# One transformer layer on one core: three groups of blocks, each group's mixer woven into the expert gathers of the group before, and gathered tiles of 4 picks by 32 tokens

## The chip, the cores and the metric

The kernel runs on one core of a Trainium2 chip. The metric is the device time of one execution in microseconds; lower is better. The engines are named as the profile names them: PE is the matrix engine TensorE (PEld its weight loads), DVE is VectorE, ACT is ScalarE, POOL is GpSimd, SP is the engine that issues plain DMAs.

## What is computed

1024 tokens of width 1024, float32. The first half of the layer is the mixer, the second half a retrieval of single-neuron experts (PEER).

```python
mod = silu(c) @ w_ada + b_ada                        # 6 rows of 1024
h = rmsnorm(x, g1) * (1 + scale1) + shift1
qa, ka, va, qb, kb, vb, ga, gb = split(h @ w_in)
y_sb = stick_breaking_attention(qa, ka, va)          # 8 heads, strictly causal: block b reads blocks 0..b
y_sw = sliding_window_sink_attention(qb, kb, vb)     # each chunk of 64 reads itself and the one before
merged = sigmoid(ga) * (y_sb @ sb_proj) + sigmoid(gb) * (y_sw @ sw_proj)
x = x + gate1 * (merged @ w_out)
h2 = rmsnorm(x, g2) * (1 + scale2) + shift2
q = h2 @ w_q                                         # 8 heads x 2 halves of 128
s = q . sub_keys ; top 16 of 128 in each half; top 16 of the 256 sums -> 16 expert numbers, softmax gates
out_t = sum over 8 heads x 16 picks of gate * gelu(h2_t . U[e]) * V[e]     # U, V: 16384 x 1024
x = x + gate2 * out ; final rmsnorm
```

U and V lie side by side in memory (`uv`), so one pick of one token is one row of 8 KB. 1024 tokens x 128 picks x 8 KB are 1074 MB.

## The kernel before

The work stands in stages, one after the other, each for all 8 blocks of 128 tokens: modulation and first norm; stick-breaking attention, a loop over 4 pairs of heads (lines 340 to 510); sliding-window attention (lines 530 to 700); gates, branch projections and merging (to line 773); output projection, residual, second norm and the store of the residual x1 (to line 871); then the experts.

In the stick-breaking loop a chunk is one block of keys against up to 512 later tokens. TensorE makes scores (L462, L466), VectorE splits them into a positive part and a magnitude (L401, L407), ScalarE takes exp and ln (L367, L369), VectorE adds (L418) and keeps a running sum (L429, L432), TensorE adds suffix sums in PSUM (L490, L495), ScalarE takes exp (L377), and TensorE multiplies by the values (L474). Six banks and `AHEAD = 4` keep several chunks under way.

The experts' stage is a loop over the 8 heads. In one turn 128 gathers are made, one for each block b and pick k: POOL's indirect DMA (L950) brings, for the 128 tokens of block b, each token's own row of 8 KB into one of `RING = 8` buffers, a token to a partition. VectorE multiplies the U half by h2 and sums (L1187, `dot`), ScalarE takes the gelu (L1055) and makes a 128x128 diagonal matrix of gate times gelu (L1044, L1060), TensorE multiplies that diagonal with the V half, 1024 columns, and adds up in PSUM (L994):

```python
pe.wait_ge(diag_done, LED + t * PICKS + n + 1)
for i in range(2):
    m = pe.matmul(pb[:, 4 + 2 * (b % 2) + i, :], dg[:, n % 4, :],
                  ring[:, n % RING, D + i * HALF:D + (i + 1) * HALF], start=(k == 0), stop=(k == TOPK - 1))
m.then_inc(ring_free, 1)
```

`ring_free` lets POOL issue the gather that is 8 further on. After 16 picks VectorE adds the block's sum to `acc` (L1176). Between the gathers of head t stand, by a list of fixed places, the keys of head t+1: 32 query matmuls (L966), scores (L975), the top 16 of 128 for 8 blocks and 2 halves (L1097 to L1105, five instructions each), the 256 sums and their top 16, and the decoding of the expert numbers. Head 0's keys stand ahead of the loop (L1007 to L1171). At the end a short stage adds x1 and makes the last norm (L1273, L1284).

Every engine runs its instructions in the order written and waits on semaphores; most stages are hardware loops.

## Time and profile before

| | |
|---|---|
| median of 2 runs | 4077.22 us (4073.49 to 4080.95) |
| span of the profiled execution, first to last instruction | 4068.1 us |
| ahead of the first gather's product | 1347.7 us |
| 1024 gathers and their sums | 2680 us |
| behind them | 40 us |
| busy share of the span | PE 83%, DVE 54%, ACT 27%, POOL 30% |

The profiled execution's span is 9.1 us under the median of the runs; what lies around the span (launch and end) is in the runs' time alone. The first 1347.7 us move few bytes and are TensorE's; the rest moves 1074 MB and keeps the DMA engines full. A busy share over the whole span mixes the two.

### The profile page before, as it was taken

The page shows a single profiled execution, that of the slowest core. Times are in us where ns is not written, and L with a number is a line of the kernel's source. Part 1 is how long each engine was busy: PE and PEld are TensorE (multiplying, and loading weights), DVE is VectorE, ACT ScalarE, POOL GpSimd, SP SyncE. Part 2 cuts the span into 40 slices and gives each one's busy share as a digit, 9 for nine tenths or more (in the row PEclk, how much of TensorE's full clock was granted, in tenths as well). Part 3 has the DMA queues.
Part 4 walks back from the last instruction along what each step waited for, and adds up shares of the span by engine and source line. Part 5 has one row for each costly group of instructions (what it writes and reads, how often), then busy time and mean ns, then how long its engine had stood idle before and what let it go on. Part 6 is the DMA issues. An engine that isn't in the chain of part 4 may idle for free. (4 is left out here: it accounts for less than half of the span.)

```text
span 4068.1 us, 34945 instructions
## 1 busy us (share of the span) xinstructions
PE 3381.3 (83%) x8576; PEld 1494.4 (37%) x8576; DVE 2195.0 (54%) x4545; ACT 1102.9 (27%) x3167; POOL 1206.8 (30%) x1050
## 2 busy tenths in 40 slices
PE   8999999799994777788697788778779778877775
PEld 3444445544442333333242333333324233332321
DVE  2233442310135677478558657747856865765555
ACT  1233330200011223333332332333333232332322
POOL 0000001200001344344344434434435443443442
PEclk9999998999997899998999999999999899999998
DMA  7100000110011799999999999999999999999997
GB/s 312 60 16 0 15 11 0 73 47 31 17 71 77 293 393 408 388 412 392 411 379 400 421 390 399 411 386 409 399 407 396 395 422 384 388 414 414 421 421 323
DMA packets 160296, 1159.90 MB, mean 285 GB/s; under 512 B 17985, under 2 KB 19025, under 8 KB 24689
## 3 DMA queue, kind: packets, MB, share of 16 engines
q0 software_dynamic: 147696, 1074.80, 64.7%
q1 hardware_dynamic: 12418, 83.40, 5.3%
q14 instruction: 156, 1.28, 0.1%
q8 instruction: 26, 0.43, 0.0%
HBM read 1149.74 MB, written 8.39 MB: 285 GB/s over the span
## 5 line engine op out<-in xcount | busy, mean ns | idle before, releaser
L994 PE MATMUL pb<-arena,dg 128*128 128x512 f32 x4096 | 1982.7, 627 | 578.3 <-ACT dg L1060 573.7
L1187 DVE CUSTOM_DVE_ANT_0 arena<-arena 128x1024 f32<-128x1024 f32 x1024 | 1239.4, 1222 | 792.4 <-DMA arena<-in_uv,idx_cur 757.7
L950 POOL DMA_INDIRECT arena<-in_uv,idx_cur x1024 | 1154.4, 1127 | 1609.4 <-PE pb L994 1406.0
L994 PEld LDWEIGHTS pb<-arena,dg 128*128 128x128 f32 x4096 | 785.4, 199 | 1722.0 <-issue 882.3
L1055 ACT ACTIVATE gl<-dots 128x2 f32<-128x2 f32 x512 | 104.0, 203 | 1630.0 <-DVE dots L1187 1624.6
L1060 ACT ACTIVATE dg<-idg,gl 128x128 f32<-128x128 f32 x1024 | 361.7, 395 | 136.3 <-PE pb L994 81.0
L1044 ACT ACTIVATE idg<-ident,gate_cur 128x128 f32<-128x128 f32 x1024 | 346.7, 387 | 0.2
L966 PE MATMUL pb<-arena 128*128 128x512 f32 x448 | 234.4, 605 | 6.0 <-DMA sks<-in_sk 6.0
L741 PE MATMUL pb<-arena 128*128 128x512 f32 x512 | 223.9, 599 | 7.3 <-DMA arena<-in_w_mg 7.3
L770 DVE TENSOR_TENSOR arena<-arena,pb 128x512 f32<-128x512 f32 x32 | 22.0, 687 | 320.4 <-PE pb L748 320.4
L548 POOL MEMSET arena<- 128x512 f32 x1 | 0.5, 524 | 596.8 <-POOLq L345 596.8
L941 POOL MEMSET arena<- 128x8192 f32 x1 | 6.9, 6924 | 477.1 <-POOLq L793 477.1
L741 PEld LDWEIGHTS pb<-arena 128*128 128x128 f32 x512 | 98.4, 192 | 131.1 <-issue 131.1
L966 PEld LDWEIGHTS pb<-arena 128*128 128x128 f32 x448 | 87.1, 195 | 116.1 <-issue 116.1
L446 PE MATMUL pb<-arena 128*128 128x512 f32 x256 | 112.6, 601 | 1.6 <-ACTq L93 1.6
L821 PE MATMUL pb<-arena 128*128 128x512 f32 x256 | 111.1, 593 | 2.6 <-PEq L722 2.6
L748 PE MATMUL pb<-arena 128*128 128x512 f32 x256 | 111.2, 592 | 0.0
L391 DVE COPY arena<-pb 128x512 f32<-128x512 f32 x8 | 5.5, 691 | 194.2 <-PE pb L455 194.2
L286 PE MATMUL pb<-arena 128*128 128x512 f32 x192 | 90.8, 629 | 12.5 <-DMA arena<-in_w_ada 12.5
L401 DVE TENSOR_SCALAR arena<-pb 128x512 f32<-128x512 f32 (+2 forms) x96 | 53.5, 557 | 83.2 <-PE pb L466 48.7
L1176 DVE TENSOR_TENSOR arena<-arena,pb 128x1024 f32<-128x1024 f32 x64 | 77.9, 1217 | 28.2 <-PE pb L994 28.1
L377 ACT ACTIVATE arena<-pb 128x512 f32<-128x512 f32 (+2 forms) x96 | 47.1, 490 | 168.8 <-PE pb L495 135.5
(166 smaller groups left out, 2473.4 us busy)
## 6 DMA issues: line engine op xcount, KB each, us to landing
arena<-in_w_ada SPq DMA_DIRECT2D x12, 2048.0 KB, 12.3
arena<-in_uv,idx_cur POOLq DMA_INDIRECT x1024
arena<-in_w_mg SPq DMA_DIRECT2D x8, 1536.0 KB, 6.3
arena<-in_w_q SPq DMA_DIRECT2D x8, 1024.0 KB
arena<-in_w_sb SPq DMA_DIRECT2D x4, 1536.0 KB, 6.2
arena<-in_x SPq DMA_DIRECT2D x1, 4096.0 KB, 24.4
arena<-in_w_out SPq DMA_DIRECT2D x1, 4096.0 KB, 19.6
arena<-in_x SPq DMA_DIRECT2D x8, 512.0 KB, 7.1
```

The source lines that it names most:

```text
L286: pe.matmul(pb[:, j % 4, :], cb[:, k, :], w[:, k, :], start=(k == 0), stop=False)
L446: m = pe.matmul(pb[:, i, :], wsb[:, i // 2, k, :], hT[:, k, (i % 2) * HALF:(i % 2 + 1) * HALF], start=(k == 0), stop=(k == KT - 1))
L741: m = pe.matmul(pb[:, q, :], wmg[:, u, (q // 2) * KT + k, :], hT[:, k, (q % 2) * HALF:(q % 2 + 1) * HALF], start=(k == 0), stop=(k == KT - 1))
L748: m = pe.matmul(pb[:, 4 + q, :], wmg[:, u, 16 + (q // 2) * 4 + k, :], y[:, k, (q % 2) * HALF:(q % 2 + 1) * HALF], start=(k == 0), stop=(k ...
L821: m = pe.matmul(pb[:, 2 * (b % 2) + i, :], mergedT[:, k, b * P:(b + 1) * P], wout[:, k, i * HALF:(i + 1) * HALF], start=(k == 0), stop=(k ...
L950: pool.indirect_dma_start(ring[:, n % RING, :], None, uv, bass.IndirectOffsetOnAxis(ap=idx_cur[:, n:n + 1], axis=0)).then_inc(gathered[n % ...
L966: m = pe.matmul(pb[:, half, :], wq[:, p, k, :], h2T[:, k, half * HALF:(half + 1) * HALF], start=(k == 0), stop=(k == KT - 1))
L994: m = pe.matmul(pb[:, 4 + 2 * (b % 2) + i, :], dg[:, n % 4, :], ring[:, n % RING, D + i * HALF:D + (i + 1) * HALF], start=(k == 0), stop=( ...
L1044: act.activation(idg[:, n % 4, :], ident[:], ACT.Copy, scale=gate_cur[:, n:n + 1]).then_inc(idg_done, 1)
L1055: act.activation(gl[:, 0:2], dots[:, n % RING:n % RING + 2], ACT.Gelu).then_inc(gelu_done, 1)
L1060: act.activation(dg[:, m % 4, :], idg[:, m % 4, :], ACT.Copy, scale=gl[:, m - n:m - n + 1]).then_inc(diag_done, 1)
L1187: dve.tensor_tensor_reduce(u, h2[:, b, :], u, 1.0, 0.0, ALU.mult, ALU.add, dots[:, n % RING:n % RING + 1]).then_inc(dots_done, 1)
```

## The change

The 8 blocks are split in three groups of 2, 3 and 3 blocks (`GROUPS`). The mixer, the keys and the norm of a group are made for that group alone (256 or 384 tokens wide). Group 0's mixer runs ahead; group 1's is woven into the gathers of group 0's experts, group 2's into the gathers of group 1's; group 2's gathers have nothing beside them but their own top-16 work. The keys and values of the stick-breaking heads of earlier groups go to memory and are read back (`k_dram`, `v_dram`), as do x1, h2 and the modulation rows.

The weaving is written out: nothing is a hardware loop any more. The engines' programs are generated by Python generators that yield at the same points on every engine. A slot is half a quad, that is 2 gathered tiles; `slots_at` deals the 144 pieces of group 1's mixer over 108 slots and the 168 pieces of group 2's over 172 slots, in proportion to the costs in `plan`, and leaves the last `LEAD = 20` slots of each group free. In the plan's proportions group 1's mixer has 3.2 slots for the norm, 37.4 for the stick-breaking heads (40 chunks), 13.8 for the window, 21.3 for the merge, 11.9 for the output and 20.6 for the queries; group 2's has 4.3, 74.7 (64 chunks), 18.9, 29.4, 16.3 and 28.3.

The weights are read in 66 parts of 512 KB (128x1024) for each group, so three times in all, plus 48 parts of `w_ada` once. Ahead of the gathers 14 parts fit in the ring's buffers (`EARLY`), later 4 (`LATE`).

A gathered tile now holds 4 picks of 32 tokens. Its sum needs a 128x32 matrix in place of the 128x128 diagonal, and 4 matmuls of 256 columns, each into another 32 of PSUM's 128 partitions, so into another group of 32 columns of TensorE's array. VectorE's product needs the 32 tokens' h2 four times over (`h2r`, by 16 DMAs a block, `copies`). The tokens' expert numbers and gates must be spread over partitions (`shf`, 16 small copies on ScalarE for each 2 heads) and the 128x32 masks are made 32 at a time on VectorE (`gm`). The ring has 10 buffers.

Two places show the weaving. On PE, in the stick-breaking part of group 1's mixer, names: `wts` the 128x32 weights of a tile, `negones`, `tri` the suffix sums, `zone` the mixer's scratch. Before, in the gathers of a turn's start:

```order
L966 MATMUL pb<-arena 128x512
L992 REGISTER_ALU
L994 MATMUL pb<-arena,dg 128x512 x2
L966 MATMUL pb<-arena 128x512
L992 REGISTER_ALU
L994 MATMUL pb<-arena,dg 128x512 x2
```

Now, one quad (two slots) there:

```order
L841 MATMUL pb<-ring,wts 32x256 x16
L639 MATMUL pb<-zone,tri 128x256
L643 MATMUL pb<-zone,negones 128x128
L629 MATMUL pb<-zone 128x384
L652 MATMUL pb<-zone 64x128
L639 MATMUL pb<-zone,tri 128x384
L643 MATMUL pb<-zone,negones 128x256
L652 MATMUL pb<-zone 64x256
L639 MATMUL pb<-zone,tri 128x384
L643 MATMUL pb<-zone,negones 128x384
L652 MATMUL pb<-zone 64x384
L841 MATMUL pb<-ring,wts 32x256 x16
```

Where one query matmul stood between two picks' sums, three chunks stand between two quads' sums (16 matmuls), and each of their suffix sums waits for VectorE.

On DVE at the same place, before (products of the gathers, then one top 16 between two products):

```order
L1187 ISA arena,dots<-arena 128x1024
L1187 ISA dots 128x1
L1109 ISA
L1097 MAX arena<-arena 128x8
L74 ISA
L1099 MAX_INDEX kidx<-arena 128x8
...
```

Now (two products a slot; `zone` as above, L1232 is the softplus, L1245 and L1248 the running sum, L1219 and L1225 the positive part and magnitude of the chunk three further on):

```order
L1485 ISA ring,dots<-h2r,ring 128x1024
L1485 ISA dots 128x1
L1485 ISA ring,dots<-h2r,ring 128x1024
L1485 ISA dots 128x1
L1232 TENSOR_TENSOR zone<-zone 128x384
L1245 TENSOR_TENSOR zone<-zone 128x384
L1219 TENSOR_SCALAR zone<-pb 128x256
L1225 SCALAR_TENSOR_TENSOR zone<-zone,pb 128x256
L1485 ISA ring,dots<-h2r,ring 128x1024
L1485 ISA dots 128x1
L1485 ISA ring,dots<-h2r,ring 128x1024
L1485 ISA dots 128x1
```

L1219 reads scores that TensorE makes only behind the suffix sum that L1232 releases, and the next slot's products stand behind L1225.

The diff, cut to what the prediction speaks of:

```diff
-PICKS = NB * TOPK
-RING = 8
+GROUPS = ((0, 2), (2, 5), (5, 8))
+RING = 10
+TILES = 4
+QUARTERS = 4
+WBUFS = 8
+EARLY = 14
+LATE = 4
+ZBANKS, AHEAD, DEEP = 4, 3, 5
+LEAD = 20
...
+def plan(g):
+    n = blocks_of(g)
+    wide = n / 3.0
+    out = [2.0] * (n + 1) + [3.0] * (n + 1)
+    for t in range(SB_PAIRS):
+        out += [4.0 * wide] * 3 + [4.5 * wide] * (2 * GROUPS[g][1]) + [2.0]
+    out += [4.5 * wide] * 6 + [4.0] * sw_slots(g)
+    out += [5.5 * wide] * 24 + [3.0]
+    out += [5.5 * wide] * 8 + [4.5] * n + [2.0] + [4.5] * n + [2.0]
+    out += [7.5 * wide] * 16 + [5.0, 5.0]
+    return out
+def slots_at(g):
+    w = plan(g)
+    span = blocks_of(g - 1) * HEADS * QUARTERS * 2 - LEAD
+    total, out, done, sofar = sum(w), [], 0, 0.0
+    for h in range(span):
+        until = total * (h + 1) / span
+        k = 0
+        while done < len(w) and sofar + w[done] <= until + 1e-6:
+            sofar += w[done]
+            done += 1
+            k += 1
+        out.append(k)
...
-        pool.wait_ge(ring_free, t * PICKS + n + 1)
-        apart(pool, pool_steps)
-        pool.indirect_dma_start(ring[:, n % RING, :], None, uv,
-                                bass.IndirectOffsetOnAxis(ap=idx_cur[:, n:n + 1], axis=0)).then_inc(gathered[n % RING], 16)
+            need(pool, ring_free, n - RING + 1)
+            col = q * 8 + (h - first) * 4 + i
+            apart(pool, pool_steps)
+            pool.indirect_dma_start(ring[:, n % RING, :], None, uv,
+                                    bass.IndirectOffsetOnAxis(ap=idx4[:, piece % 2, col:col + 1], axis=0)
+                                    ).then_inc(gathered[n % RING], 16)
...
-        pe.wait_ge(diag_done, LED + t * PICKS + n + 1)
-        for i in range(2):
-            m = pe.matmul(pb[:, 4 + 2 * (b % 2) + i, :], dg[:, n % 4, :],
-                          ring[:, n % RING, D + i * HALF:D + (i + 1) * HALF], start=(k == 0), stop=(k == TOPK - 1))
-        m.then_inc(ring_free, 1)
+def add_up(n):
+    b, k = n // PER_BLOCK, n % PER_BLOCK
+    h, q, i = k // PER_HEAD, k % PER_HEAD // TILES, k % TILES
+    pe.wait_ge(w_done, n + 1)
+    if h == 0 and i == 0 and q % 2 == 0 and b:
+        pe.wait_ge(acc_act if q == 0 else acc_dve, 8 * b)
+    for f in range(4):
+        m = pe.matmul(pb[32 * f:32 * f + 32, 6 + q // 2, (q % 2) * 256:(q % 2 + 1) * 256], wts[:, n % WBUFS, :],
+                      ring[:, n % RING, D + 256 * f:D + 256 * (f + 1)],
+                      start=h == 0 and i == 0 and q % 2 == 0, stop=h == HEADS - 1 and i == TILES - 1, skip_group_check=True)
+    m.then_inc(ring_free, 1)
...
+for s in spans(merge(0), output(0), queries(0)):
+    pass
+for g in range(NG):
+    a, b = GROUPS[g]
+    background = mixer(g + 1) if g + 1 < NG else None
+    rate = slots_at(g + 1) if g + 1 < NG else None
+    for at in range((b - a) * HEADS * 8):
+        quad = a * HEADS * 4 + at // 2
+        if at % 2 == 0 and quad:
+            for i in range(TILES):
+                add_up(TILES * (quad - 1) + i)
+        if background is not None:
+            for _ in range(rate[at]):
+                next(background)
...
-    act.activation(idg[:, n % 4, :], ident[:], ACT.Copy, scale=gate_cur[:, n:n + 1]).then_inc(idg_done, 1)
-        act.activation(gl[:, 0:2], dots[:, n % RING:n % RING + 2], ACT.Gelu).then_inc(gelu_done, 1)
-        act.wait_ge(gelu_done, t * (PICKS // 2) + n // 2 + 1)
-        act.wait_ge(idg_done, t * PICKS + n + 2)
-        for m in (n, n + 1):
-            act.wait_ge(ring_free, t * PICKS + m - 3 + RING)
-            act.activation(dg[:, m % 4, :], idg[:, m % 4, :], ACT.Copy, scale=gl[:, m - n:m - n + 1]).then_inc(diag_done, 1)
+    tables(GELU)
+    act.wait_ge(dots_done, n + 4)
+    act.wait_ge(gm_done, piece + 1)
+    link(act.activation(gl[:, quad % 2, :], dots[:, n % 16:n % 16 + 4], ACT.Gelu))
+    need(act, ring_free, n + 4 - WBUFS)
+    for i in range(TILES):
+        act.activation(wts[:, (n + i) % WBUFS, :], gm[:, piece % 2, col + i, :], ACT.Copy, scale=gl[:, quad % 2, i:i + 1]).then_inc(w_done, 1)
...
+    elif k == 12:
+        act.wait_ge(sel_done, piece + 1)
+        for q in range(QUARTERS):
+            for j in range(TILES):
+                src = sel[32 * q:32 * q + 32, :, :].rearrange("p x (n j) -> p x n j", j=4)[:, :, 0:4 * nh, j]
+                op = act.activation(shf[32 * j:32 * j + 32, piece % 2, :, q, 0:4 * nh], src, ACT.Copy)
+        op.then_inc(shuffled, 1)
...
-        if b and n % TOPK == 4:
-            add_block(t, b - 1, not keys)
-        if keys:
-            for p in range(2):
-                if TOP_AT[p] <= n < TOP_AT[p] + NB:
-                    top_half(t + 1, p, n - TOP_AT[p])
-            if n == CAND_AT:
-                candidates(t * 2 + 4)
-            if BEST_AT <= n < BEST_AT + 2 * NB and (n - BEST_AT) % 2 == 0:
-                top_pairs((n - BEST_AT) // 2)
-            if DECODE_AT <= n < DECODE_AT + 13:
-                decode(None, n - DECODE_AT)
-            if n == DECODE_AT + 22:
+        for i in range(2):
+            dot(TILES * quad + 2 * (at % 2) + i)
+        if hq == 1 and blk:
+            drain(blk - 1)
+        if hq in (2, 3, 4) and blk:
+            final(blk - 1, hq - 2)
+        for piece, k in steps.get(at, ()):
+            step(piece, k)
+        if background is not None:
+            for _ in range(rate[at]):
+                next(background)
+drain(NB - 1)
+for k in range(3):
...
+def copies(b, q):
+    need(sp, dots_done, b * PER_BLOCK - (QUARTERS - 1 - q) * TILES)
+    i, g = place_of(b)
+    need(sp, h2_out[i], 16 * uses_of(i, g))
+    for j in range(TILES):
+        sp.dma_start(h2r[32 * j:32 * j + 32, q, :], h2_dram[b * P + 32 * q:b * P + 32 * q + 32, :]).then_inc(in_h2r[q], 16)
...
-        "w_ada": a["w_ada"][0].reshape(KT, P, 12, HALF).transpose(2, 1, 0, 3),
+        "w_all": np.concatenate([w_sb, wq, wkv, w_mg, w_out, w_q], axis=0),
+        "w_ada": a["w_ada"][0].reshape(4, 2, P, ADA_HALVES, HALF).transpose(3, 0, 2, 1, 4).reshape(4 * ADA_HALVES, P, D),
```

In `plan`, the costs are in arbitrary units. ScalarE reloads its function tables by `tables(...)`, in the gathers of a mixed group mostly twice a quad (gelu, then exp and ln).

## Rows read from the trace of the kernel before

**Rows 1.** The page's slices: 40 equal stretches of the span, tenths

```profile
PE   8999999799994777788697788778779778877775
DMA  7100000110011799999999999999999999999997
```

**Rows 2.** Busy time by stage: stretch, length, engines (instructions), granted clock, DMA share, GB/s

```profile
128.00:600.00 472.00, 467.23 (x1568) 220.42 (x1568) 194.11 (x440) 154.18 (x313) 0.00 (x0) 0.99 0.04 16
...
685.00:775.00 90.00, 68.07 (x488) 61.45 (x486) 53.00 (x59) 32.04 (x56) 42.27 (x16) 0.83 0.00 1
...
1285.00:1348.00 63.00, 2.07 (x2) 0.50 (x2) 51.42 (x167) 2.09 (x4) 7.59 (x8) 0.50 0.33 134
1348.00:3600.00 2252.00, 1835.56 (x4076) 769.55 (x4077) 1509.55 (x3259) 701.83 (x2221) 972.77 (x850) 0.95 0.98 398
3600.00:4026.00 426.00, 325.60 (x683) 128.19 (x681) 234.67 (x371) 128.28 (x426) 174.04 (x166) 0.97 1.01 417
```

**Rows 3.** The gathers' products by stretch: all heads but the last, then the last

```profile
L1187 DVE CUSTOM_DVE_ANT_0 arena<-arena x853: 1202/1224/1298, 1347.7 to 3596.9; 128x1024 f32<-128x1024 f32 x171
...
L1187 DVE CUSTOM_DVE_ANT_0 arena<-arena x171: 1216/1226/1283, 3601.5 to 4025.8; 128x1024 f32<-128x1024 f32 x171
```

**Rows 4.** Weight loads at the start, windows with the same columns as Rows 2

```profile
20.00:40.00 20.00, 17.50 (x36) 7.09 (x36) 0.37 (x2) 11.66 (x20) 0.00 (x0) 0.91 1.00 410
```

**Rows 5.** Groups of instructions: busy us, mean ns | idle before, releaser

```profile
L994 PE MATMUL pb<-arena,dg 128*128 128x512 f32 x4096 | 1982.7, 627 | 578.3 <-ACT dg L1060 573.7 <-issue 3.9
L446 PE MATMUL pb<-arena 128*128 128x512 f32 x256 | 112.6, 601 | 1.6 <-ACTq L93 1.6
L455 PE MATMUL pb<-arena 128*128 128x128 f32 x512 | 60.2, 280 | 0.0
L966 PE MATMUL pb<-arena 128*128 128x512 f32 x448 | 234.4, 605 | 6.0 <-DMA sks<-in_sk 6.0
L1055 ACT ACT_TABLE_LOAD x14 | 18.0, 1283 | 0.2
```

**Rows 6.** Timeline, stick-breaking: suffix sums of a chunk, next scores, their split

```profile
303.70 1.13 PE L490 MATMUL pb<-arena,tri 128*128 128x512 f32 x2
...
304.66 1.02 PE L495 MATMUL pb<-arena,negones 128*128 128x512 f32 x2
...
305.61 0.91 PE L462 MATMUL pb<-arena 64*128 64x384 f32 x2
...
306.72 0.56 DVE L401 TENSOR_SCALAR arena<-pb 128x384 f32<-128x384 f32 x1 [1.61 <-PE pb L466]
...
307.33 0.55 DVE L407 SCALAR_TENSOR_TENSOR arena<-arena,pb 128x384 f32<-128x384 f32 x1
```

**Rows 7.** Timeline: two top-16 passes of 128, then of 256 values begin

```profile
1310.16 0.28 DVE L1097 MAX8 arena<-arena 128x8 f32<-128x128 f32 x1
...
1312.31 0.28 DVE L1097 MAX8 arena<-arena 128x8 f32<-128x128 f32 x1
...
1324.55 0.43 DVE L1097 MAX8 arena<-big 128x8 f32<-128x256 f32 x1
...
1327.71 0.41 DVE L1097 MAX8 arena<-big 128x8 f32<-128x256 f32 x1
```

**Rows 8.** Timeline, one block of the window: its scores, then the bias

```profile
706.38 4.37 PE L605 MATMUL pb<-arena 64*128 64x192 f32 x16
...
710.79 1.76 DVE L689 SCALAR_TENSOR_TENSOR arena<-pb,big 128x1536 f32<-128x1536 f32 x1 [5.08 <-PE pb L605]
```

**Rows 9.** L629's burst: 64 columns of the array, then the other 64; timeline, then matmuls in flight

```profile
744.96 3.33 PE L629 MATMUL pb<-arena 128*64 128x128 f32 x32 [1.34 <-ACT arena L657]
...
744.96 3.09 PEld L629 LDWEIGHTS pb<-arena 128*64 128x64 f32 x32 [1.58 <-ACT arena L657]
...
745.50:745.55 0.05, 0.05 (x3) 1.00 0.00 0
746.55:746.60 0.05, 0.05 (x6) 1.00 0.00 0
```

2241 lines of the change are left out of this document (1224 added, 1017 removed).

## The prediction

> **What bounds the kernel now.** Read the slices first [rows 1]: for the first third of the span DMA is near zero and PE near full, then DMA stands at nine or more and stays there. So there are two kernels in a row, and a busy share over the whole span says nothing. Next the stages [rows 2]. Up to the first product at 1347.7 us [rows 3] TensorE works (467 of 472 us in the stick-breaking loop) while 16 GB/s are moved; only in the last 63 us is it idle, behind VectorE's top-16 work. From there the DMA engines are 98 to 101% busy at 398 to 417 GB/s. TensorE is busy for 1836 of 2252 us there too, but it isn't the bound: in the last head, with no keys beside the gathers, it falls to 326 of 426 us and the pace hardly moves. The pace itself: 170 intervals from 3601.5 to 4025.8 us give 2.496 us for a gather; with keys beside them 853 took 2254 us, 2.64 each [rows 3]. Bytes decide, and the mixer runs while no bytes do. 40 us follow for the last norm.
>
> **What the change takes off the path.** Of the 1348 us ahead, only group 0's share (2 blocks of 8) and what can't be divided stay. A TensorE instruction of 512 columns takes 112.6/256 = 0.44 us, one of 128 takes 60.2/512 = 0.118 [rows 5]; on that line 256 columns take 0.225 and 384 take 0.332 (both estimates). Group 0:
> - modulation of shift and scale, x, transposes: 16 parts and x are 9.4 MB, at 410 GB/s [rows 4] 23 us, with some 25 us of start and latencies: 48.
> - stick-breaking, 4 pairs: 32 instructions of 256 and 32 of 128 columns are 11 us; four short chunks in a dependent chain some 15. 104 in all.
> - window: projections 22, and two blocks. The old stage had 90/8 = 11 us a block with two blocks overlapped [rows 2]; now nearly all is in sequence. Scores to bias 4.4 us and the bias 1.76 [rows 8], a reduction and a scaling of the same width, exp, two rounds of transposes: 20, between 11 and 23. 60.
> - the other 32 modulation parts: 18 aren't prefetched, 23 us of bytes: 35.
> - merge: 8 x 48 instructions x 0.225 = 86. Output: 32 matmuls of 512 columns, two instructions each, 28, and 15 for two norms: 43.
> - queries: VectorE's top 16 of 128 takes 1312.31 - 1310.16 = 2.15 us [rows 7]; 32 of them, 69, more than TensorE's 16 x 3.6: 75.
> - the first two heads' 256 sums (2 x 3.16 [rows 7]), decoding, spreading over partitions, landing: 26.
> Sum 477, taken as 475, in place of 1348. Behind the last product: one block's drain, gate, residual, norm (four VectorE passes over 1024 columns, 1.22 us each [rows 3], two of ScalarE) and a store: 15 in place of 42.
>
> **What it adds to the DMA engines.** For groups 1 and 2 each: 66 parts 34.6 MB; x twice, x1, h2 7.5; rows and table 2.3; keys and values 2.6; sub-keys 1; h2 four times over 2 MB a block, x1 and out 1 MB a block. That is 52.5 MB beside group 0's 256 gathers, 55 beside group 1's 384, 9 beside group 2's. At 2.496 us and 410 GB/s: 639 + 128 = 767; 958 + 134 = 1092; 958 + 22 = 980; together 2839.
>
> **What it adds to the sums.** A tile's 8 instructions (4 matmuls, two each) of 256 columns are 1.8 us in a row, about what 1982.7/1024 is now [rows 5]. If four column groups work side by side, 0.45. The trace has one place that tells: L629 writes columns 0 to 63 of the array for four heads, then 64 to 127. 32 instructions of 107 ns or more should need 3.6 us, and they took 3.33; where one half takes over from the other, 6 are in flight in place of 3 [rows 9]. So I take 0.45. Here the Trainium skill speaks against the change: "TensorE: Matmul & The Clock Gate", Part 3, says that weight loads overlap running matmuls only if their row group differs, and here all 4 have the same 128 rows. By that, the sums would come near to the 1.8 in a row. The trace does not agree: L629's loads, same rows, lie within its matmuls (3.09 us of loads inside 3.33) [rows 9].
>
> **What it adds in waits.** This is the large term. All engines now pay a slot's pieces in the same order. A slot's gathers take 2 x 2.496 = 4.99 us of DMA; VectorE's two products, 1.224 each [rows 3] and slightly overlapped, take 2.3. The rest of the slot must hold the background's chains, and VectorE's next products stand behind them. In stick-breaking, from the suffix sums to the split of the chunk three further on, 306.72 - 303.70 = 3.0 us pass at 512 columns [rows 6]; at 384 some 2.35. With the softplus ahead and the split behind (0.56 and 0.55 for passes of this width [rows 6]) a full chunk holds VectorE for 4.1 us, the running sum in its shadow; with the narrow ones 3.74 on average in group 1, 3.87 in group 2. Their bounds are 1.66 (VectorE's own work, all waits hidden) and 5.5 (one of ScalarE's table loads, 1.28 [rows 5], in every chain too); the row is of this same chain, so I stay near it. A pair's start costs 20 (projections 32 x 0.332 + 48 x 0.118 = 16.3, and three scores with their exp and ln). The top-16 work of a piece of 2 heads is about 15 us of VectorE each 16 slots.
> Beside group 0's gathers, chain in us: norm 30; stick-breaking 40 x 3.74 + 30 slots x 2.3 + 28 + 4 x 20 = 327 (DMA alone would take 209); window 32 + 60 + 15 = 107; merge 24 x 16 x 0.332 = 127, with sums 148 (DMA 137); output 88; queries 48 x 2.15 + 47 + 19 = 169 (DMA 145); the free 20 slots 100. 969, less 25 that a full ring of 10 buffers makes good once: 940, in place of DMA's 767.
> Beside group 1's: 35; 64 x 3.87 + 148 + 60 + 80 = 536; 115; merge 178, DMA's; 110; 103 + 65 + 27 = 195; 110. 1279, less 25: 1250, in place of 1092.
> Group 2's: 980, DMA's; VectorE has 470 of products and 180 of top 16.
>
> **Sum.** 475 + 940 + 1250 + 980 + 15 = 3660 against the span of 4068.1. The median of the runs lies 9.1 above that span, so 3669. Its own range, with chunks at 3.0 to 5.0 us, a window block at 11 to 23, and the start at 440 to 530, is 3540 to 3830.
>
> **Rivals.**
> *The waits are hidden.* Chunks overlap products, the ring evens out the stages, and bytes alone decide: 475 + 2839 + 15 + 9 = 3338. For it: VectorE's own work leaves room. Beside group 0's gathers it is 294 of products, 120 of pieces and some 240 of mixer, norm and keys, 654 of 767; beside group 1's 442, 180 and 285, 907 of 1092. Against: VectorE is strictly in order, and before it, too, the pace fell from 2.496 to 2.64 as soon as keys stood between products [rows 3]. Chance 0.20.
> *The sums go one after another.* 1.35 us more a tile. In 145 slots of stick-breaking and window 2.7 a slot, of which 1.4 hides under the products: 189. In 50 merge slots 2.7, less some slack: 113. 3669 + 302 = 3970. This is also what the Trainium skill's rule on weight loads, above, would give. Chance 0.05.
> *Plain loads queue behind the gathers.* If a part waits for the 10 gathers ahead of it (25 us, 4 parts under way: 6.2 us a part), parts that are wanted each 3.3 to 4.8 us come late: 50 parts x 2 groups x 3 us: 3970. Against: over 448 instructions of L966, which need such loads, TensorE waited for DMA 6 us in all [rows 5]. Chance 0.10.
> *Slower: TensorE's clock.* Gaps while VectorE multiplies can drop the granted clock to its lower level, 1.2 GHz, as in the 63 idle us (0.50), and in part in the window stage, busy 68 of 90 us (0.83); in dense stages it is 0.99 [rows 2]. All of TensorE's work on the path would double: chunks 104 x 2.0 = 208, pair starts 130, windows 104, merges 280, outputs 84, queries 40: 846, so 4515 in full. It ties with the old kernel at 48% of that time, a mean of 0.76, and is 2% slower at 58%, a mean of 0.71. Against: in the mixed stages TensorE would still be busy for 60% and more with gaps under 2.3 us. Chance 0.12, half of it past 4159.
>
> **How the numbers follow.** 0.48 for the forecast, 0.20, 0.05, 0.10, 0.12 for the rivals, 0.05 for what I don't see. The forecast and most rivals are faster: 0.86. Within 2% (3996 to 4159; that is about what a measurement of this kernel can tell from no change) 0.06, slower 0.08. The range of 8 in 10 reaches from 3400, where part of the waits is hidden, to 3930, with some of the clock or the queue; below and above lie about 0.1 each.
>
> **What would show it.** First product near 475 us; the product of group 0's last tile some 940 us later, group 1's 1250 after that, the last 384 tiles at 2.5 to 2.55 us each. DMA share about 0.8 in the first two stretches and 1.0 in the last. VectorE's largest wait in stick-breaking is for L629 or L632. A tile's 8 sum instructions start within 0.5 us. If the DMA share is 1.0 throughout, the first rival holds; if the tile takes 1.8 us, the second; if VectorE waits for weights through TensorE, the third; a granted clock below 0.8 is the fourth. I would be most wrong if a wait across engines in a stage other than stick-breaking (the window's, above all) lasts longer than its slots.

## The result, and the profile after

The changed kernel takes 3873.23 us (median of 2 runs, 3872.2 to 3874.26), the one before 4077.22: a ratio of 0.950, with a 95% interval of 0.947 to 0.953. The forecast was 3669. It had the direction; the gain was to be 408 us and is 204. The profiled execution's span is 3872.5 us, 1.8 us under its own time of 3874.26. In the other runs, too, a time lies about 2 us above its own span, so most of the 9.1 us between the old kernel's median and its profiled span was a difference between executions, and not launch and end.

The page of the changed kernel, its slices [rows 1]:

```profile
PE   7788567786987643677677888766433333333333
...
PEclk8889878885998866777777789878755655656556
DMA  5263577774899889787787899998899999999997
```

From the sixth slice on DMA is at 7 to 9 tenths while a mixer is woven in (4 in one slice), at 9 once the last group's gathers are alone. The products of the gathers, by stretch [rows 3] (shortest, median and longest ns, first and last start):

```profile
L1485 DVE CUSTOM_DVE_ANT_0 ring<-h2r,ring x256: 1194/1221/1248, 481.6 to 1497.6; 128x1024 f32<-128x1024 f32 x128
...
L1485 DVE CUSTOM_DVE_ANT_0 ring<-h2r,ring x384: 1204/1221/1236, 1500.2 to 2852.1; 128x1024 f32<-128x1024 f32 x192
...
L1485 DVE CUSTOM_DVE_ANT_0 ring<-h2r,ring x384: 1218/1226/1294, 2854.6 to 3853.6; 128x1024 f32<-128x1024 f32 x192
```

So 481.6 us ahead of the first product, 1018.6 for group 0's stretch, 1354.4 for group 1's, 999.0 for group 2's, 18.9 behind. The stretches can be cut further at the first TensorE instruction of each part of the mixer, as the window's first projections here (group 1's mixer begins its window at 834.8, group 0's at 140.4):

```profile
L694 PE MATMUL pb<-hT,wst x160: 486/486/590, 834.8 to 2152.6; 128*128 128x384 f32 x160
...
L694 PE MATMUL pb<-hT,ring x80: 379/379/454, 140.4 to 157.5; 128*128 128x256 f32 x80
```

Busy time by these parts, columns as in [rows 2] with VectorE, ScalarE and POOL behind PE and PEld. Beside group 0's gathers: stick-breaking, window, merge, queries, free slots; then the same five beside group 1's; then group 2's alone:

```profile
515.00:835.00 320.00, 247.30 (x1257) 124.62 (x1257) 185.63 (x408) 133.68 (x307) 79.06 (x75) 0.81 0.71 271
835.00:979.00 144.00, 110.66 (x569) 61.42 (x569) 67.21 (x128) 40.21 (x114) 31.85 (x29) 0.72 0.62 240
979.00:1130.00 151.00, 148.33 (x737) 83.14 (x736) 78.60 (x151) 55.67 (x134) 46.74 (x41) 0.99 0.98 373
1228.00:1400.00 172.00, 123.36 (x676) 72.40 (x672) 135.11 (x502) 33.18 (x103) 46.40 (x44) 0.88 0.84 333
1400.00:1500.00 100.00, 32.96 (x296) 12.74 (x300) 58.64 (x115) 20.77 (x77) 43.17 (x36) 0.59 0.93 353
1542.00:2123.00 581.00, 416.75 (x2057) 186.55 (x2058) 363.91 (x763) 254.28 (x561) 166.93 (x151) 0.76 0.76 292
2123.00:2260.00 137.00, 110.63 (x632) 61.69 (x632) 82.54 (x154) 45.84 (x140) 48.36 (x41) 0.76 0.82 331
2260.00:2441.00 181.00, 159.97 (x864) 87.56 (x864) 99.06 (x199) 59.28 (x152) 65.68 (x57) 0.95 1.01 400
2557.00:2755.00 198.00, 135.44 (x808) 77.47 (x800) 159.49 (x552) 43.95 (x140) 63.95 (x60) 0.85 0.88 349
2755.00:2854.00 99.00, 31.14 (x292) 12.09 (x296) 59.25 (x115) 20.35 (x76) 43.13 (x36) 0.60 1.00 382
2854.00:3853.00 999.00, 344.36 (x3072) 132.90 (x3072) 623.38 (x1212) 201.33 (x726) 444.80 (x378) 0.59 1.01 410
```

The merges run at the DMA engines' limit (0.98 and 1.01). DMA is emptiest in group 0's window (0.62), then in the two stick-breaking parts (0.71 and 0.76) and in the second window (0.82). In the windows TensorE waits for a fifth to a quarter of the time at a mean granted clock of 0.72 to 0.76, between its two levels (1.2 and 2.4 GHz). Beside the forecast, with its terms:

| part, us | forecast | measured | more |
|---|---|---|---|
| ahead of the first product | 475 | 481.6 | 7 |
| group 0: norm; stick | 30; 327 | 33.0; 320.2 | -4 |
| window | 107 | 143.8 | 37 |
| merge; output | 148; 88 | 151.0; 98.7 | 14 |
| queries and 20 free slots | 269 | 272.0 | 3 |
| full ring's credit | -25 | 0 | 25 |
| group 1: norm; stick | 35; 536 | 41.6; 581.0 | 52 |
| window | 115 | 137.1 | 22 |
| merge; output | 178; 110 | 181.4; 115.8 | 9 |
| queries and 20 free slots | 305 | 297.4 | -8 |
| full ring's credit | -25 | 0 | 25 |
| group 2; behind it | 980; 15 | 999.0; 18.9 | 23 |

That is 205 us. The forecast rounded its two woven sums down from 944 and 1254 to 940 and 1250, which makes it 213, and 8 come off again because the profiled execution lies 1 us under the median and not 9.

### The profile page after: what moved, and what is told of

Its sections match the earlier page's. It is cut to its first block and busy times, and to the rows that moved or that the text cites. A ratio compares the mean times of both kernels' runs of the same rounds, so it can differ in the third digit from the quotient of the medians.

```text
span 3872.5 us, 40886 instructions
## 1 busy us (share of the span) xinstructions
PE 2395.4 (62%) x13784; PEld 1252.0 (32%) x13784; DVE 2247.4 (58%) x5130; ACT 1071.6 (28%) x2946; POOL 1173.2 (30%) x1033
## 5 line engine op out<-in xcount | busy, mean ns | idle before, releaser
L558 POOL DMA_INDIRECT ring<-in_uv,idx x1024 | 1170.1, 1143 | 2666.6 <-PE pb L841 1992.9
L1485 DVE CUSTOM_DVE_ANT_0 ring<-h2r,ring 128x1024 f32<-128x1024 f32 x1024 | 1233.1, 1223 | 669.6 <-DMA ring<-in_uv,idx 603.2
L841 PE MATMUL pb<-ring,wts 128*32 128x256 f32 x8192 | 774.5, 544 | 976.5 <-ACT wts L1093 971.3
L841 PEld LDWEIGHTS pb<-ring,wts 128*32 128x32 f32 x8192 | 317.1, 149 | 1433.4 <-ACT wts L1093 1112.9
L884 ACT ACT_TABLE_LOAD x220 | 282.3, 1283 | 4.6 <-PEq L1628 0.7
L639 PE MATMUL pb<-zone,tri 128*128 128x384 f32 (+2 forms) x240 | 127.7, 624 | 236.5 <-DVE zone L1232 236.3
L1093 ACT ACTIVATE wts<-gm,gl 128x32 f32<-128x32 f32 x1024 | 245.1, 310 | 8.3
L821 PE MATMUL pb<-zone,wst 128*128 128x384 f32 (+1 forms) x768 | 236.8, 463 | 0.8 <-issue 0.8
L1219 DVE TENSOR_SCALAR zone<-pb 128x384 f32<-128x384 f32 (+2 forms) x120 | 57.3, 478 | 226.1 <-PE pb L629 137.6
L767 PE MATMUL pb<-hT,wst 128*128 128x384 f32 x512 | 173.5, 496 | 3.6 <-ACT ys L1007 3.6
L821 PEld LDWEIGHTS pb<-zone,wst 128*128 128x128 f32 x768 | 146.1, 195 | 82.1 <-issue 17.5
L639 PEld LDWEIGHTS pb<-zone,tri 128*128 128x128 f32 x240 | 47.4, 247 | 300.1 <-DVE zone L1232 291.1
L629 PE MATMUL pb<-zone 64*128 64x384 f32 (+2 forms) x240 | 124.3, 606 | 8.1 <-issue 7.5
L660 PE MATMUL pb<-hT,wst 128*128 128x384 f32 x256 | 87.9, 499 | 7.7 <-ACT hT L918 7.5
```

The costliest lines, as they stand in the source:

```text
L558: pool.indirect_dma_start(ring[:, n % RING, :], None, uv, bass.IndirectOffsetOnAxis(ap=idx4[:, piece % 2, col:col + 1], axis=0)).then_inc( ...
L629: m = pe.matmul(pb[:, (base + c) % ZBANKS, 0:hi - lo], kT[64 * e:64 * e + 64, s * P:(s + 1) * P], qT[64 * e:64 * e + 64, lo:hi], start=Tru ...
L639: m = pe.matmul(pb[:, bank, 0:hi - lo], tri[:], spl[(base + c) % DEEP][:, 0:hi - lo], start=False, stop=True, skip_group_check=True)
L767: m = pe.matmul(pb[:, 4 * (u % 2) + i, 0:t_], w[:, k, :], ht[:, k, :], start=k == 0, stop=k == KT - 1)
L821: o = pe.matmul(pb[:, m % 2, 0:t_], w[:, k, :], ht[:, k, :], start=k == 0, stop=k == KT - 1)
L841: m = pe.matmul(pb[32 * f:32 * f + 32, 6 + q // 2, (q % 2) * 256:(q % 2 + 1) * 256], wts[:, n % WBUFS, :], ring[:, n % RING, D + 256 * f:D ...
```

## Experiments

Each was timed together with the kernel before, whose medians were 4068 to 4074 us. Stretches are from first product to first product, as above.

**A chunk's scores ahead of the suffix sums of an earlier one** (stick-breaking, TensorE's order alone):

```diff
+                            if c + AHEAD < len(chunks):
+                                scores(c + AHEAD)
                             suffix(c)
-                            if c + AHEAD < len(chunks):
-                                scores(c + AHEAD)
```

> In the stick-breaking part TensorE makes the scores of the chunk three further on before the suffix sums of the present chunk, not behind them. Theory A (the missing time is VectorE's wait for scores that stand behind the suffix sums it has just released): VectorE's waits for L629 and L632, 225 us in the changed kernel, nearly vanish, a chunk gets about 1.2 to 1.8 us shorter, 104 chunks, so 3873 falls to 3690 to 3750. Theory B (the missing time is TensorE's low clock, 0.81 and 0.76 in the two stretches): TensorE's work is on the path in any order, so under 40 us are gained, 3835 or more. If bytes bound these stretches, nothing changes.

3694.45 us (4 runs), ratio 0.908 (0.906 to 0.910). Theory A holds. Stretches 966.0, 1229.1 and 999.3. The two stick-breaking parts, in this kernel:

```profile
507.00:780.00 273.00, 226.39 (x1256) 117.53 (x1256) 184.38 (x408) 131.62 (x307) 85.39 (x75) 0.89 0.82 321
...
1483.00:1939.00 456.00, 361.10 (x2056) 169.03 (x2056) 361.34 (x764) 249.84 (x561) 180.40 (x151) 0.86 0.95 372
```

The same instructions take 273 us in place of 320 and 456 in place of 581. VectorE's waits for the next scores, in the changed kernel and then in this one (us in total, times, longest):

```profile
DVE zone L1219 <- PE pb L629: 137.6, 56, 3.9
...
DVE zone L1219 <- PE pb L632: 87.7, 53, 4.8
```

```profile
DVE zone L1219 <- PE pb L632: 31.2, 35, 3.6
...
DVE zone L1219 <- PE pb L629: 16.6, 15, 2.7
```

They fall from 225 to 48 us, by 177, and the kernel is 179 us faster. What goes is this, in the timeline of the changed kernel (start, duration, engine; in brackets the idle time before it and its releaser; L639 and L643 are the suffix sums, L629 the next scores, L1219 their split):

```profile
698.12 0.91 PE L629 MATMUL pb<-zone 64*128 64x384 f32 x2
...
703.65 0.42 DVE L1232 TENSOR_TENSOR zone<-zone 128x256 f32<-128x256 f32 x1
...
704.12 1.22 PE L639 MATMUL pb<-zone,tri 128*128 128x256 f32 x2 [5.09 <-DVE zone L1232]
...
705.13 0.64 PE L643 MATMUL pb<-zone,negones 128*128 128x128 f32 x2
...
705.70 1.65 PE L629 MATMUL pb<-zone 64*128 64x384 f32 x2
...
707.38 0.56 DVE L1219 TENSOR_SCALAR zone<-pb 128x384 f32<-128x384 f32 x1 [2.80 <-PE pb L629]
```

TensorE stood 5.09 us for a softplus (L1232) behind two products and a mask of the gathers; then VectorE stood 2.80 us until the suffix sums and the scores behind them were through, at half the clock (granted 0.50 from 704 to 707 us; L629 takes 1.65 us here and took 0.91 at 698.12, at 1.00). With the scores ahead, the split has its input before the softplus is asked for, and VectorE doesn't wait for it.

**Sums in one column group** (2 matmuls of 512 columns a tile in place of 4 of 256):

```diff
-                    for f in range(4):
-                        m = pe.matmul(pb[32 * f:32 * f + 32, 6 + q // 2, (q % 2) * 256:(q % 2 + 1) * 256], wts[:, n % WBUFS, :],
+                    for f in range(2):
+                        m = pe.matmul(pb[32 * q:32 * q + 32, 6 + f, :], wts[:, n % WBUFS, :],
```

> A tile's sum goes by two matmuls of 512 columns into one group of 32 columns of the array (the group is that of the tile's 32 tokens), not by four of 256 columns into four groups. If the four groups work side by side and that hides the sums: a tile needs 1.8 us of TensorE at full clock in place of 0.45, and where chains bound the slots some 200 to 350 us are lost, 4070 to 4220; the last stretch (384 tiles, nothing beside them) stays at 2.6 us a tile if the clock rises, and goes to 3.5 if it stays at half. If the groups didn't work side by side, no change, 3873.

4274.83 us (2 runs), ratio 1.050 (1.048 to 1.053), above the range expected; stretches 1185.0, 1587.3, 999.5, the last one unchanged with its clock raised, as expected. The columns streamed are the same, and TensorE is busy for 670 of 900 us in the last stretch at a clock of 0.92, 1.94 us a tile:

```profile
3300.00:4200.00 900.00, 669.98 (x1382) 154.74 (x1383) 0.92 1.01 411
```

In the changed kernel four tiles take 3.64 us in the same stretch, 0.91 us each. The stretch's mean clock is 0.59, but in this burst the granted clock is 0.50, so that is 0.45 us a tile at the full clock (an estimate). The four column groups do work side by side, and that is worth 402 us: without it the change would be slower than the kernel before.

```profile
2909.65 3.64 PE L841 MATMUL pb<-ring,wts 128*32 128x256 f32 x32 [6.44 <-ACT wts L1093]
```

**Matmuls that add zeros** between the mixer's steps, to see what the low clock costs (2 in a chunk's step, 4 in one of the window, 5 in each slot of 2 tiles, in 54 of 64 slots):

```diff
+                def fill(k):
+                    for _ in range(k if warm[0] and 8 <= warm[1] <= 61 else 0):
+                        pe.matmul(pb[:, 7, 0:P], ident[:], zero[:].to_broadcast([P, P]), start=False, stop=True, skip_group_check=True)
...
+                            fill(2)
...
+                        fill(4)
...
+                        fill(5)
```

> TensorE gets idle work that adds zeros to a bank of the sums, in the stick-breaking and window parts beside the gathers: 5 matmuls of 128 columns at each slot's start, 2 after each chunk, 4 after each window piece, in 54 of 64 slots. Nothing else moves. Theory B (low clock): the granted clock of these parts, 0.72 to 0.81, rises to 0.95 or more and the time falls by 60 to 150 us although TensorE does more, 3720 to 3810. Theory A (order of the chain) alone: within 30 us of 3873, or slower if the filler delays suffix sums.

3903.14 us (4 runs), ratio 0.959 (0.958 to 0.961). Over the windows of the changed kernel's parts the clock rose to 0.88 and 0.87 (group 0's stick-breaking and window) and to 0.86 and 0.90 (group 1's),

```profile
515.00:835.00 320.00, 282.02 (x1645) 174.60 (x1643) 173.59 (x384) 123.33 (x278) 74.00 (x71) 0.88 0.68 259
```

and the stretches are 1030.0, 1370.4 and 997.4, the first two 11 and 16 us longer than without. Cut at their own projections, the stick-breaking parts take 336 and 586 us in place of 320 and 581. The run is outside theory B's range and within theory A's 30 us. It doesn't show what the low clock costs by itself, since the added matmuls stand in the same order as the work and take time too; the narrower test is further down.

**Nothing woven** (each group's mixer by itself, between the gathers):

```diff
-                    background = mixer(g + 1) if g + 1 < NG else None
+                    background = None
+                    if g:
+                        for s in mixer(g):
+                            pass
```

> Groups and tiles as changed, but no weaving: each group's mixer runs between the gathers of the group before and its own. If the weaving hides the mixers as forecast: 482 + 650 (256 tiles) + 660 (mixer of 3 blocks alone) + 980 + 740 + 980 + 18, about 4510, so weaving is worth some 640 us and the change would lose without it. If the weaving gave little (chains so long that they might as well stand alone): 4000 to 4100.

4701.24 us (1 run), above both expectations and nearer the first: the two mixers took 707 and 829 us where 660 and 740 were reckoned, the gathers the rest. Gathers alone take 662, 1001 and 998 us for the three groups, 2.59 to 2.61 us a tile; the mixer alone 707 (group 1) and 829 (group 2). Woven they took 1019 in place of 1369, and 1354 in place of 1830: the weaving hides 350 and 476 us. It also pays for what the split costs: in three groups the mixers take 483 + 707 + 829 = 2019 us by themselves, where all 8 blocks together took 1347.7 before, so without weaving the change loses 624 us. This trace also shows the window with nothing beside it, projections and then three blocks:

```profile
1391.70:1424.00 32.30, 31.39 (x128) 20.62 (x128) 1.90 (x5) 1.47 (x3) 0.00 (x0) 1.00 0.33 106
1424.00:1519.00 95.00, 65.63 (x217) 34.87 (x217) 18.67 (x27) 19.91 (x67) 0.00 (x0) 0.54 0.02 6
```

A block costs 95/3 = 32 us, with no gather to blame. The clock is 1.00 in the projections and 0.54 in the blocks.

**The window's slots filled** (onto the first edit: 12 matmuls that add zeros in each of three slots a block, nowhere else):

```diff
+                        if any(1 <= s - 4 * i <= 3 for i in range(n)):
+                            fill(12)
```

> The kernel with a chunk's scores ahead of the previous suffix sums (3694 us), and in the sliding window's slots of groups 1 and 2 twelve more matmuls of 128x128 by a slot, which add zeros to the sums' bank in the time in which TensorE waits for the softmax. Theory A (a block of the window takes 32 us instead of the 20 forecast because TensorE, which waits between scores, flips and mixes, is granted .72 to .76 of its clock there and does its own short steps at 1.2 GHz): the granted clock of the window's stretches rises to .85 or more and the two windows go from 142 and 137 us to 120 to 125, the median to 3655 to 3675. Theory B (the chain of score, bias, maximum, exponential, transpose and value product is long by its hand-overs on VectorE and ScalarE, the clock is only a sign of it): the clock rises and the windows stay at 135 to 150 us, the median at 3685 to 3715.

3678.6 us (4 runs), ratio 0.903 (0.901 to 0.904), against 0.908 without.

```profile
786.50:918.60 132.10, 119.43 (x784) 79.14 (x784) 65.97 (x126) 40.01 (x114) 36.15 (x30) 0.90 0.66 258
1935.70:2066.30 130.60, 122.07 (x853) 80.74 (x849) 82.77 (x154) 46.01 (x140) 47.17 (x41) 0.92 0.86 346
```

The windows went from 142 and 137 us to 132 and 131, with the clock from 0.71 and 0.76 to 0.90 and 0.92; their stretches are 958.5 and 1224.9, only 8 and 4 us shorter. Both theories missed. At a nearly full clock the windows still are 25 and 16 us above their terms; the clock's part that this takes away is 10 and 6 us, less what the added matmuls cost.

**No table loads beside the gathers** (onto the first edit; the gathers' GELU left out, ScalarE copies):

```diff
-                    tables(GELU)
+                    tables(EXP_LN)
...
-                    link(act.activation(gl[:, quad % 2, :], dots[:, n % 16:n % 16 + 4], ACT.Gelu))
+                    link(act.activation(gl[:, quad % 2, :], dots[:, n % 16:n % 16 + 4], ACT.Copy))
```

> The kernel with a chunk's scores ahead of the suffix sums (3694 us), with the GELU of the gathered products left out: ScalarE copies them instead, so that its tables need not be exchanged between the gathers' GELU and the mixer's exponential and logarithm (220 table loads of 1283 ns, 282 us of ScalarE, go to some 20). It leaves the GELU out of the output. Theory A (TensorE and VectorE set the pace of a chunk; ScalarE's 282 us of table loads stand beside them): the median stays within 3660 to 3700. Theory B (a chunk's chain goes through ScalarE's softplus, which waits behind the table load after a GELU, so about one load a chunk, 1.28 us for the 76 and 138 chunks of the two sticks, is on the path): up to 214 chunks x 1.28 = 270 us less, of which the gathers' own floor lets at most some 200 through: 3490 to 3600.

3681.38 us (4 runs), ratio 0.904 (0.902 to 0.906), against 0.908 (0.906 to 0.910). 60 table loads are left of 220, not some 20, so 160 are gone. ScalarE is busy 856 us in place of 1066, and about 13 us of that come through, hardly more than the noise. The two stick-breaking parts take 273 and 457 us, as with the loads. Theory A, for the kernel with the scores ahead; with the old order it was not tried.

**Groups of 3, 3 and 2 blocks** (onto the first edit):

```diff
-GROUPS = ((0, 2), (2, 5), (5, 8))
+GROUPS = ((0, 3), (3, 6), (6, 8))
```

> The kernel with a chunk's scores ahead of the suffix sums (3694 us), with groups of 3, 3 and 2 blocks instead of 2, 3 and 3. The part that nothing covers at the start grows by one block and the gathers that nothing shares at the end shrink by one. Theory A (a stretch lasts as long as its mixer needs when that is longer than its gathers, and the last group's gathers alone take 2.6 us a tile): prologue some 715 us (alone, the mixer of three blocks took 707), stretch of group 0 with 384 tiles over the mixer of group 1 some 1130, stretch of group 1 with 384 tiles over a mixer of two blocks with longer prefixes some 1060 to 1100, last 256 tiles 665, tail 18: 3590 to 3630. Theory B (woven gathers and mixer share the bandwidth and TensorE, so only the total of work counts and a longer prologue, in which no tile is gathered, is a loss): 240 us more of prologue against 333 us less of last gathers, and the two woven stretches keep their 2195 us: 3600 at best, and up to 3700 if the second stays at the 1229 of three blocks.

3685.56 us (4 runs), ratio 0.905 (0.903 to 0.906): as good as no gain over 0.908. First product at 670.2, stretches 1197, 1142, 661. The start grew by 194 us and the rest of the span shrank by 195. The time is in theory B's range, but not for its reason: the two woven stretches were to keep their 2195 us and have 2339. Over the time that their gathers need alone (1001 us for 384 tiles, 662 for 256), the woven stretches have 196 and 141 us more; with groups of 2, 3 and 3 it was 304 and 228. More gathers for each block of mixer hide more of it, but what is gained so is paid for ahead of the first product.

**A ring used as if it had six buffers** (the changed kernel):

```diff
-                                need(pool, ring_free, n - RING + 1)
+                                need(pool, ring_free, n - 6 + 1)
```

> The changed kernel as it is (3873 us), but GpSimd starts a tile's gather only when the tile six before it is used up, instead of ten: the ring of gathered rows is four buffers shorter. Theory A (a full ring carries nothing over the free slots: the credit of 25 us a group that the prediction took for ten filled buffers does not exist, because gathers are issued at the pace of use and the stretch waits for them anyway): 3865 to 3900, within 1% of the changed kernel. Theory B (the ring covers the stretches in which TensorE and the queues are busy with the merge and the output; four buffers of 2.6 us each at each of the four or five such places is 40 to 50 us, more if the gathers stop while the sums wait): 3915 to 4000.

4424.18 us (4 runs), ratio 1.086 (1.084 to 1.088). Both theories were far off: stretches 1122.4, 1567.7 and 1231.5. Even with nothing beside the gathers,

```profile
3173.00:4404.00 1231.00, 343.36 (x3068) 132.08 (x3059) 625.31 (x1212) 200.88 (x723) 422.01 (x382) 0.57 0.87 332
```

a tile takes 3.21 us. POOL's gathers there, from 3300 to 3800 us, and the time from issue to landing:

```profile
L558 POOL DMA_INDIRECT ring<-in_uv,idx x156: 932/938/1990, 3305.2 to 3796.6; - x156
...
  PE pb L841: 303.2, 75
...
DMA to landing us min/median/max: 5.4/7.2/11.1
```

POOL waits 303 of 500 us for the sums to give a buffer back; with ten buffers it is 242 of the same 500 us. My reading: a quad's sums start only when all four of its products are made, so up to four buffers are held by the quad in work, and what is left must cover the 7.2 us to landing. Then the ring is no store of finished tiles; nearly all of it is in flight or in work. In the changed kernel's long stick-breaking part POOL waits the same way, 382.7 us of 581, a larger share than with gathers alone; with the scores ahead it is 241.3 of 456:

```profile
L558 POOL DMA_INDIRECT ring<-in_uv,idx x151: 935/942/2001, 1541.2 to 2121.7; - x151
...
  PE pb L841: 382.7, 47
```

This fits TensorE giving buffers back late when it is held at a suffix sum, so that gathers start late.

**Six buffers with the scores ahead** (both edits):

> A chunk's scores ahead of the suffix sums, with a ring used as if it had six buffers. With the old order six buffers instead of ten made the stretches 104, 213 and 232 us longer, and the two sticks 44 and 124. Theory A (one cause: TensorE, waiting at the suffix sums, gives buffers back late, so the gathers starve; with the new order the buffers come back in time and a short ring hurts the stick no more than it does the last stretch, 0.6 us a tile): the sticks are about 273 + 30 and 456 + 92 us long, 540 to 560 in group 1 instead of 705, and the median 4190 to 4250. Theory B (two causes that add: a short ring costs every tile its latency, whatever TensorE's order): the sticks keep their +44 and +124, and the median is 3694 + 551 = 4245 or more, with group 1's stick at 575 to 600.

4363.38 us (4 runs), ratio 1.071 (1.069 to 1.074). Stick-breaking 349.5 and 657.8 us: the new order is worth 15 and 48 us where with ten buffers it was 47 and 125. Neither theory: theory A had 303 us and 540 to 560 for these parts, theory B 317 and 575 to 600. The short ring costs more in the new order (77 and 202 us) than in the old one (44 and 124). My reading, not tried further, is that the time which the early scores free is of use only if gathers can be issued ahead to fill it.

**Four groups of 2 blocks, with ten and with eleven buffers** (onto the first edit):

```diff
-GROUPS = ((0, 2), (2, 5), (5, 8))
+GROUPS = ((0, 2), (2, 4), (4, 6), (6, 8))
...
-RING = 10
+RING = 11
```

> The kernel with a chunk's scores ahead of the suffix sums (3694 us), with four groups of 2 blocks instead of 2, 3 and 3, and a ring of ten as before; it is also the measure for the kernel with one buffer more. Theory A (a stretch hides more of a mixer when it has more gathers for each block of it): each of the three woven stretches has 256 tiles over the mixer of two blocks, 760, 790 and 820 us with the longer prefixes, the last 256 tiles 665: 476 + 2370 + 665 + 18 = 3530. Theory B (tiles and mixer divide one budget of bandwidth and TensorE, as the groups of 3, 3 and 2 had it, which gained 8 us): the woven stretches keep their excess of 88 us a block over the 2.6 us a tile, and a fourth reading of the weights is added: 476 + 768 x 2.6 + 531 + 40 + 665 + 18 = 3730.

> The four groups of 2 blocks with a ring of eleven buffers instead of ten (the smaller groups leave that much room). With six buffers the changed kernel lost 551 us, 232 of them in the last stretch and 317 in the woven ones. Theory A (the woven stretches are still short of buffers, since TensorE gives a tile's buffer back late while it is in a mixer step): one buffer more brings 30 to 60 us against the same kernel with ten. Theory B (ten already cover the time from issue to landing, and what is lost in the woven stretches is bandwidth and TensorE's time): 0 to 10 us.

3744.86 and 3727.46 us (4 runs each), ratios 0.919 (0.918 to 0.921) and 0.915 (0.914 to 0.917). With ten: first product at 478.8, stretches 821, 860, 904, 661. Over the 661 of its last stretch, gathers alone, the woven ones are 160, 199 and 243 us longer, 602 together, where three groups had 532. The woven stretches also got 128 tiles more, 333 us that the end no longer has, so in all nothing is saved and 50 us are lost: theory B. The edit adds a fourth reading of the weights; how much of the 50 us that is was not measured. The eleventh buffer brings 17 us, all in the woven stretches (the last is 660 with both), between the two theories.

**9 free slots in place of 20** at the end of a stretch (onto the first edit, onto the four groups with eleven buffers, and onto the groups of 3, 3 and 2):

```diff
+REST = 9
...
-    span = blocks_of(g - 1) * HEADS * QUARTERS * 2 - LEAD
+    span = blocks_of(g - 1) * HEADS * QUARTERS * 2 - REST
```

> The kernel with a chunk's scores ahead of the suffix sums (3694 us), with the mixer spread over all slots of the group before but the last 9, instead of all but the last 20. Theory A (the free slots are a loss: in them nothing of the mixer is hidden, 11 slots or 22 tiles more for it in each of the two woven stretches are 22 x 2.6 = 57 us each, of which what the mixer already takes at the margin is most): 60 us less or more, 3600 to 3640. Theory B (the slots stretch by what is woven into them wherever it stands, so the same work at a thinner pace costs the same, and the free slots let the ring fill and the next group's first choice be ready): 3680 to 3710.

> The four groups of 2 blocks with a ring of eleven and 9 free slots at a stretch's end instead of 20. Theory A (free slots are a loss): 3 x 30 = 90 us under the kernel with eleven buffers and 20 free slots. Theory B (only the sum of work counts): within 20 us of it.

> Groups of 3, 3 and 2 blocks with a chunk's scores ahead of the suffix sums (3686 us) and 9 free slots instead of 20. Theory A (free slots are a loss wherever a mixer stands in front of them): 40 to 60 us less, 3625 to 3645. Theory B (with 384 tiles over two blocks the second stretch is near its gathers' floor of 2.6 us a tile already, only the first gains): 20 to 30 us less, 3655 to 3665.

3641.6 us, ratio 0.893 (0.892 to 0.895); 3670.75, 0.900 (0.899 to 0.902); 3664.67, 0.901 (0.898 to 0.903), 4 runs each. That is 53, 57 and 21 us less than with 20. Free slots are a loss, but not everywhere: in the first of the three kernels the first stretch goes from 966.0 to 927.1 us and the second only from 1229.1 to 1226.4 (its two profiled executions differ by 40 us, the medians by 53). With four groups the woven stretches are 20, 22 and 1 us shorter, with 3, 3 and 2 blocks 16 and 13. Why the second stretch of the first kernel gains next to nothing is open. The first time is at the edge of theory A's range; the second is between its theories; the third is in theory B's range, though the stretch that was not to gain gave 13 of the 29 us.

**The three edits that helped, together** (scores ahead, 9 free slots, the window's slots filled):

> Three edits together: a chunk's scores ahead of the suffix sums, 9 free slots instead of 20 (3642 us with these two), and twelve matmuls that add zeros in each of the window's slots (16 us less when added to the first edit alone). Theory A (the edits take different waits away, their gains add): 3620 to 3632. Theory B (the stretches are near the floor of their gathers, so a gain in the window is given back in the slots behind it): 3636 to 3650.

3627.43 us (4 runs), ratio 0.891 (0.889 to 0.893), the fastest. The last step is 14 us (3641.6 to 3627.4), as theory A has it, though the two were timed apart and the intervals of their ratios (0.892 to 0.895 and 0.889 to 0.893) overlap at the edge. Its stretches are 917.6, 1215.5 and 996.0.

## Why the prediction was right and where it was wrong

**Right: the mechanism and most terms.** The mixer moves under the gathers, the woven stretches run slower than their bytes, and the rest of a slot is VectorE in order behind chains that cross engines. The start (475 for 481.6), group 0's stick-breaking (327 for 320.2), both merges (148 and 178 for 151.0 and 181.4) and both spans of queries with free slots (269 and 305 for 272.0 and 297.4) are within 3%. VectorE's largest waits in stick-breaking are for L629 and L632, as said: 147 us in group 1's part and 71 in group 0's, where the projections (L666) follow with 54. The DMA share is 0.81 and 0.86 in the woven stretches and 1.01 in the last, where about 0.8 and 1.0 were forecast. The tile's sums take 0.45 us at the full clock, though 0.91 at the half clock that they mostly run at in the last stretch; the one-group kernel shows the price of the other case. The reading from one burst [rows 9] was thin: 32 instructions of 107 ns are 3.42 us and not 3.6, so 3.33 us was only 3% under a row of single instructions, and the six in flight were the better sign. The rule of the Trainium skill that was held against it ("TensorE: Matmul & The Clock Gate", Part 3: loads overlap only another row group) does not hold for four column groups with the same rows: 0.91 us a tile at a clock of 0.50 against 1.94 at 0.92, reckoned by clocks a factor of 3.9 (an estimate). Nor was it all that this Part of the Trainium skill says: its table has three column tiles at 2.38 times the speed, which speaks for the change.

**The step that failed: "Beside group 0's gathers, chain in us" and the line on group 1's**, as sizes. Three terms of them make up 154 of the 205 us.

*"Window: ... 20, between 11 and 23" for a block.* It is 32 with nothing beside it, past the upper bound; 59 us of the miss, 37 and 22 in the two stretches. I had the scores and the bias from [rows 8], and for the reductions, exp and transposes a round figure. The lower bound came from a stage in which two blocks overlapped at a clock of 0.83 [rows 2]; in the new order the blocks follow one another and the clock is 0.54 in them. TensorE is busy for 66 of the 95 us there; at the full clock that would be 36 us by estimate (66 x 0.54), 10 us less for each block. In the woven kernel filling the slots took off 10 and 6 us for three blocks. How the remaining excess divides between hand-overs and the clock's rest was not measured. Where the prediction named the place in which it would be most wrong, it named the window, and left the number as it was.

*"Less 25 that a full ring of 10 buffers makes good."* It gave nothing, twice: 50 us. In the 20 free slots VectorE still waits for the DMA before half of its products, in the changed kernel between 1400 and 1500 us:

```profile
L1485 DVE CUSTOM_DVE_ANT_0 ring<-h2r,ring x39: 1219/1225/1227, 1399.0 to 1497.6; 128x1024 f32<-128x1024 f32 x39
...
  DMA ring<-in_uv,idx: 32.2, 20
```

39 products take 100 us, the DMA's own pace, so the ring held no ten landed tiles. The runs with six buffers fit this: four buffers fewer lengthen even the last stretch by 232 us, as if nearly all were in flight or in work. The free slots were counted nearly right, at 100 and 110 us for 100 and 99; the credit against them was an idea with no row behind it.

*Group 1's stick-breaking, "64 x 3.87".* 581.0 us less the terms for products, pieces and starts (148, 60 and 80) is 293 for 64 chunks, 4.6 us each; group 0's 40 are 143, or 3.6, against 3.74. One price for both was wrong by 45 us in the longer part. With the scores ahead the two come to 2.4 and 2.6 us by the same subtraction, so TensorE's order made up a third of it in group 0's part and two fifths in group 1's. ScalarE's table loads, which the bound of 5.5 reckoned with, are no part of what is left in the new order (without 160 of them 13 us in all, none of it in these parts). Why group 1's chunk costs a full us more than group 0's in the old order stays open. A little under half of it is there without any gathers: with nothing woven the two parts take 232 and 351 us, which less the starts' 80 is 3.8 and 4.2 us a chunk. Its clock is lower, 0.76 against 0.81, but a kernel with its clock raised was no faster; and the short ring cost it more, 124 us for 152 tiles against 44 for 75.

*Smaller:* both outputs 17 (group 0's 11 more), both norms 10, the start 7, and group 2's stretch 19: 2.60 us a tile, where the forecast of 980 has 2.55 (2.496 from the last head before, and 9 MB of other bytes). The rate is 410 GB/s against 417 before [rows 2], and 1.7% of 999 us is 17 us, nearly all of it. The gathers alone show the same 2.6 and one buffer more doesn't change it, so neither the mixer nor the ring is the cause of the lower rate; what is, was not tried.

**The rivals.** *Waits hidden* did not come true, but from 3873 to 3627 us its direction was open by edits of a few lines. *Sums one after another* fell with the one-group kernel. *Plain loads queue behind gathers*: no. The page's group in which TensorE waited longest for weights, and for comparison VectorE's largest wait of the mixer:

```profile
L1219 DVE TENSOR_SCALAR zone<-pb 128x384 f32<-128x384 f32 (+2 forms) x120 | 57.3, 478 | 226.1 <-PE pb L629 137.6
...
L787 PE MATMUL pb<-wst,zone 128*128 128x512 f32 x192 | 91.3, 633 | 18.7 <-DMA wst<-in_w_all 18.7
```
 
*TensorE's clock*: the mean granted clock is 0.746, below the 0.8 that was to be this rival's sign and below the 0.76 at which I had it tie with the old kernel, and the kernel is 5% faster. The rule that took a mean for the whole was wrong: the clock is low where TensorE isn't asked for much, 0.59 in the last 999 us, which cost nothing (with one column group it is 0.92 there and the stretch 999.5 us), and high (0.95 to 0.99) in the merges, where the matmuls are the work. In stick-breaking, where VectorE does wait for TensorE, it is 0.81 and 0.76, and what that costs is not shown: the run that raised it added work of its own.
